# An encoder layer on one core: two blocks of the program made one, norm roots of eight token tiles taken ahead, and the last 32 tokens multiplied in four column tiles

## The chip, the cores and the metric

The kernel runs on one core of a Trainium2 chip. The metric is the device time of one execution in microseconds (us); lower is better. The hardware profiler recorded one execution, from which all rows below are taken.

## The reference, cut to what matters

Two sequences, a prompt of 256 tokens and a sample of 1024, each get 16 learned tokens in front and pass through one layer. All arithmetic is float32.

```
h = rmsnorm(x, norm1_g)
z = h @ w_in                      # u | q | k | v | o | gates
q, k = silu(centred_dwconv(q, k))
y_pool = pool_mixer(u)
h_f, h_b = mlstm_chunkwise forwards and backwards (q, k, v, gates)
h = (h_f + h_b) * rsqrt(mean((h_f + h_b)^2, per head) + EPS)
y_mlstm = h * mh_g * sigmoid(o)
x = x + [y_pool, y_mlstm] @ w_out
t = rmsnorm(x, norm2_g)
aff = softmax(t @ w_router); gate, idx = top_k(aff.T, cap)   # 16 experts
x = x + scatter_add(gate * ((silu(t[idx] @ w_gate) * (t[idx] @ w_up)) @ w_down))
return rmsnorm(x, final_g)
```

There are 4 heads of 192 columns, worked on in two passes of a pair (384 columns) each.

## The kernel before, in words

The two sequences lie one behind the other: 272 + 1040 = 1312 tokens (`LEN`), in `NT` = 11 tiles of 128 (`P`). Ten tiles are full; the last one, tile 10, has 32 tokens, and all products treat it as 128 wide. The order of the work is written out by hand, engine by engine; the engines meet at semaphores. The banks 0 to 2 of PSUM are handed out in turn by `bank_plan` (L75): whoever needs the next bank waits until the one that had it three places before is read out.

The program has three blocks, and at the end of a block every engine waits for all others.

**The first block** (L388 to L1169) has the input norm, the products with `w_in` and the two passes. On TensorE (PE):

- `output_gate` (L1007) multiplies each tile with the output-gate columns of the first pair and the 16 gate columns, 400 columns, 8 matmuls; `take_o` (L591) on ScalarE (ACT) copies the result, `gate_rows` (L1021) transposes the gates, and then come the products with the pool columns (L1053).
- `tokens_by_block` (L1079) gives v (and in the second pass first o) by token: for each of the 11 tiles 8 matmuls of 128 tokens by 384 columns. It stands in the program three times: v of pass 0, o of pass 1, v of pass 1. ACT copies each tile out of its bank (`evac`, L582). After v, PE waits until the last tile is read out, and starts the chain of chunk states (`transpose_keys`, `state_products`).
- Then the loop over the 11 chunks (L1136 to L1169). For each chunk VectorE (DVE) weighs the scores (L960), and PE multiplies them with v (L1167); DVE makes the hidden rows `hh` (L986, L989), ACT sums their squares (`square_hh`, L725), and GpSimd (POOL) multiplies them into `og` (L569).

After the last chunk of a pass the norm of the heads is taken for all tiles at once: ACT has summed the last squares, DVE makes the mean (L994), ACT the root (L794), DVE the reciprocal (L996):

```
square_hh(p, NT - 1)
act.wait_ge(ms_ready, p + 1)
act.activation(ss_h[:, :], ss_h[:, :], ACT.Sqrt).then_inc(rms_ready, 1)
```

**The second block** (L1172 to L1469) begins with the second pair's scaling by these reciprocals on POOL, a tile at a time in `ORDER_B` = 2, ..., 10, 0, 1 (L1207). Step n of its main loop on PE is: `project(n, 0)` (L1421, first 512 columns of the out projection, 8 matmuls of 128 by 512), the transposes of the normed tile n-1 (`transpose_t`) and of the mixer output of tile n+1 (`transpose_y`), the router logits of tile n-1 (L1418), and `project(n, 1)`. DVE adds the residual (`add`, L1281) and norms (`norm`, L1290), ACT moves transposes and squares. Between these, DVE does the rounds of the top-k search (`rank`, L1314), spread over the steps:

```
spread = {STEP_A + 1: (0, 0, 1, 5), STEP_A + 2: (0, 5, 6, 11), STEP_A + 3: (0, 11, 12, rounds),
          STEP_B + 1: (1, 0, 2, 7)}
```

with `STEP_A` = 5, `STEP_B` = 9 and `rounds` = 17. In step 8 of this table (tile 10, since `ORDER_B[8]` is 10) one round stands ahead of the add of the first half, and five ahead of the add of the second. After the loop DVE ends the search, and the rows of the first expert are gathered.

**The third block** (L1503 on) is the loop over the 16 experts. The change leaves it as it is.

Of the kernel before, what the change touches and what calls it, by code (L numbers as in the profile page):

```python
# [21 lines left out]
P = 128  # L22
D = 1024
# [10 lines left out]

GAP = 8
# [100 lines left out]
def encoder_program(nc, x_prompt, x_sample, meta, g1, w_in, conv_w, conv_b, gate_b, pool_w, pool_scale,  # L136
# [9 lines left out]
    with ctx:  # L146
# [160 lines left out]


# [79 lines left out]
        with nc.Block() as block:  # L388
# [103 lines left out]


            @block.gpsimd
            def _(pool):
# [48 lines left out]

                def mask_decay(p, i):
# [6 lines left out]
                for p in range(2):  # L552
# [17 lines left out]
                    pool.wait_ge(y_raw, (p + 1) * NT)  # L570
                    if p == 1:
                        break
                    pool.wait_ge(rs_ready, 1)
                    ogf = area("og", NT * PAIR).rearrange("p (n d) -> p n d", d=HD)
                    pool.tensor_tensor(ogf, ogf, ss_h[:, :].unsqueeze(2).to_broadcast([P, 2 * NT, HD]), ALU.mult).then_inc(y_scaled, 1)


            @block.scalar
            def _(act):
# [154 lines left out]

                gate_rows_first()
                for p in range(2):
                    for w in range(2):
# [14 lines left out]
                        if w == 0 and p:  # L752
                            act.wait_ge(y_out, 16)
                            for i in range(NT):
                                evac(("vo", p, i, 1), og[:, i, :, :], lambda b: b[:, 0:PAIR].rearrange("p (h d) -> p h d", h=2), ACT.Sigmoid)
                    if p == 0:
# [4 lines left out]
                    for i in range(NT):  # L761
                        b, k = plan[("vo", p, i, 0)]
                        if i == 0:
                            act.wait_ge(ones_set, 1)
                        evac(("vo", p, i, 0), v[:, i, :, 0:HD], lambda b: b[:, 0:PAIR].rearrange("p (h d) -> p h d", h=2))
# [5 lines left out]
                    for i in range(NT):  # L771
# [20 lines left out]
                    square_hh(p, NT - 1)  # L792
                    act.wait_ge(ms_ready, p + 1)
                    act.activation(ss_h[:, :], ss_h[:, :], ACT.Sqrt).then_inc(rms_ready, 1)  # L794


            @block.vector
            def _(dve):
                st = Steps(dve, dve_step)
                dve.memset(xin[NT - 1], 0.0).then_inc(x_clear, 1)  # L800
                dve.memset(small[:, 94:95], EPS).then_inc(eps_set, 1)
                dve.memset(gtok, 0.0).then_inc(zeroed, 1)
# [113 lines left out]

                def update_state(new, old, k0, k1, p, d, i):
# [14 lines left out]
                for p in range(2):  # L932
# [6 lines left out]
                    if p == 0:  # L939

                        b, k = plan[("rc", NT - 1)]
                        dve.wait_ge(full[b], k)
                        dve.memset(v[:, :, :, HD:VW], 1.0).then_inc(ones_set, 1)
# [6 lines left out]
                    for i in range(NT):  # L950
                        m = p * NT + i

# [870 lines left out]
```

## Time and profile before

| | |
|---|---|
| median of 3 runs | 1875.99 us (1874.95 to 1876.86) |
| the profiled execution | 1875.08 us, its span in the trace 1873.1 us |
| PE | busy 1795.1 us, 96% of the span |
| PE, weight loads | 1451.7 us, 77% |
| DVE | 472.4 us, 25% |
| ACT | 385.6 us, 21% |
| POOL | 210.5 us, 11% |
| mean granted TensorE clock | 0.981 |
| stages | first block to about 698 us, second to about 934 us, experts to the end |

How to read it: the kernel is float32, and each matmul of the program shows as two pairs of a weight load (PEld) and a matmul (PE) in the trace. A matmul's duration contains the way through the array, which the next one overlaps, so the pace of a row of matmuls is its whole time by their number. The granted clock is 1.00 at 2.4 GHz and 0.50 at 1.2 GHz. "<-" in brackets names who ended an engine's idle time, "issue" that nobody did in the records.

### The profile page before, as it was taken

Reading aid. Unit: us, or ns where it says so; the run is one execution under the profiler, and the core shown is the slowest. Engines: PE = TensorE matmul, PEld = TensorE weight load, DVE = VectorE, ACT = ScalarE, POOL = GpSimd, SP = SyncE. Lnnn points to the kernel's source line nnn. Section 1 sums busy time; section 2 is a strip of 40 time slices with the busy share of each in tenths; the row PEclk is TensorE's granted clock in tenths of the full one; section 3 lists DMA queues with packets and bytes.
Section 4 is the critical chain, followed back from the end, with each engine's and each line's share of the span. In section 5 each row is a group of like instructions: output and inputs, shape, how many; then the busy total and the mean of one; then the engine's idle time right before and its main releaser. Section 6 shows DMA issues by size and latency. Waiting matters only on the chain. (4 is left out here: it accounts for less than half of the span.)

```text
span 1873.1 us, 24252 instructions
## 1 busy us (share of the span) xinstructions
PE 1795.1 (96%) x10062; PEld 1451.7 (77%) x10062; DVE 472.4 (25%) x987; ACT 385.6 (21%) x868; POOL 210.5 (11%) x235
## 2 busy tenths in 40 slices
PE   7999999999999989999499999999999999999996
PEld 4555556955555774554299999999999999999995
DVE  3462103731020671156801101101111111111114
ACT  3335223633030551232100000000000000000005
POOL 0070010320100121000000111001110101110010
PEclk9999999999999999999689999999999999999998
DMA  6111111021100314433337686677776676876685
GB/s 193 49 48 28 40 34 40 24 85 34 34 29 1 130 44 136 170 113 131 123 123 270 218 292 223 222 245 256 249 266 218 229 269 223 283 240 214 231 283 204
DMA packets 149468, 292.28 MB, mean 156 GB/s; under 512 B 9193, under 2 KB 34457, under 8 KB 149413
## 3 DMA queue, kind: packets, MB, share of 16 engines
q1 hardware_dynamic: 142548, 269.35, 41.3%
q0 software_dynamic: 6864, 22.17, 4.7%
q8 instruction: 37, 0.61, 0.1%
q14 instruction: 19, 0.15, 0.0%
HBM read 260.20 MB, written 31.31 MB: 156 GB/s over the span
## 5 line engine op out<-in xcount | busy, mean ns | idle before, releaser
L1731 PE MATMUL bank<-arena 128*128 128x164 f32 x4096 | 581.1, 303 | 0.0
L1731 PEld LDWEIGHTS bank<-arena 128*128 128x128 f32 x4096 | 572.7, 190 | 0.3
L1750 PE MATMUL bank<-arena 128*128 128x164 f32 x2048 | 295.3, 303 | 0.0
L1750 PEld LDWEIGHTS bank<-arena 128*128 128x128 f32 x2048 | 286.5, 190 | 0.0
L1107 PE MATMUL bank<-arena 128*128 128x512 f32 (+1 forms) x576 | 215.2, 536 | 0.0
L1107 PEld LDWEIGHTS bank<-arena 128*128 128x128 f32 x576 | 110.3, 192 | 103.6 <-issue 93.6
L1640 DVE TENSOR_TENSOR arena<-bank,arena 128x328 f32<-128x328 f32 x64 | 32.0, 499 | 584.3 <-ACT arena L1580 584.3
L1085 PE MATMUL bank<-arena 128*128 128x384 f32 x528 | 171.2, 485 | 0.0
L1424 PE MATMUL bank<-arena 128*128 128x512 f32 x352 | 159.4, 611 | 1.1 <-issue 0.7
L1085 PEld LDWEIGHTS bank<-arena 128*128 128x128 f32 x528 | 99.8, 189 | 70.4
L1580 ACT ACTIVATE arena<-bank 128x328 f32<-128x328 f32 x64 | 28.4, 443 | 558.8 <-PE bank L1731 558.8
L1424 PEld LDWEIGHTS bank<-arena 128*128 128x128 f32 x352 | 67.6, 195 | 82.6 <-issue 82.4
L1546 POOL DMA_INDIRECT residual<-arena,cur_scatter x30 | 46.0, 1535 | 582.1 <-DVE arena L1648 577.5
L910 DVE SCALAR_TENSOR_TENSOR arena<-arena,par 128x272 f32<-128x272 f32 (+1 forms) x48 | 42.7, 931 | 234.9 <-ACT arena L687 234.5
L1588 ACT ACTIVATE arena<-bank 128x328 f32<-128x328 f32 x64 | 28.3, 443 | 280.1 <-PE bank L1750 280.0
L1636 DVE COPY arena<-bank 128x328 f32<-128x328 f32 x64 | 31.7, 495 | 196.5 <-PE bank L1714 196.5
L925 DVE SCALAR_TENSOR_TENSOR arena<-arena,spc,bank 128x193 f32<-128x193 f32 x120 | 42.7, 412 | 142.6 <-PE bank L1064 142.6
L1018 PE MATMUL bank<-arena 128*128 128x400 f32 x176 | 63.2, 512 | 0.7 <-DMA arena<-in_w_in 0.7
L1155 PE MATMUL bank<-arena 128*128 128x193 f32 x320 | 56.0, 326 | 0.0
L1018 PEld LDWEIGHTS bank<-arena 128*128 128x128 f32 x176 | 33.4, 195 | 24.8 <-issue 3.0
L585 ACT ACTIVATE arena<-bank 128x384 f32<-128x384 f32 (+1 forms) x50 | 25.5, 517 | 128.0 <-PE bank L1085 127.2
L1155 PEld LDWEIGHTS bank<-arena 128*128 128x128 f32 x320 | 51.8, 190 | 0.0
(210 smaller groups left out, 1427.0 us busy)
## 6 DMA issues: line engine op xcount, KB each, us to landing
arena<-in_w_up SPq DMA_DIRECT2D x32, 2048.0 KB, 12.7
arena<-in_w_down SPq DMA_DIRECT2D x32, 2048.0 KB, 10.4
arena<-in_w_gate SPq DMA_DIRECT2D x32, 2048.0 KB, 8.1
arena<-in_w_in SPq DMA_DIRECT2D x8, 1536.0 KB, 6.9
arena<-in_x_sample SPq DMA_DIRECT2D x14, 512.0 KB, 6.9
arena<-decay_rows SPq DMA_DIRECT2D x22, 256.0 KB, 3.7
residual<-arena SPq DMA_DIRECT2D x11, 512.0 KB, 5.3
ffn_in<-arena SPq DMA_DIRECT2D x11, 512.0 KB, 3.8
```

Of the source, the lines that this page charges most:

```text
L910: st.do(dve.scalar_tensor_tensor(o, Z[:, lo + n_seq + n_tap:hi + n_seq + n_tap], par[:, c0:c0 + 1], o, ALU.mult, ALU.add))
L925: last = dve.scalar_tensor_tensor(new[:, j, :], old[:, j, :], spc[:, a, i:i + 1], ps[b][:, c:c + VW], ALU.mult, ALU.add)
L1018: last = pe.matmul(ps[6 + i % 2][:, 0:OGW], hT[:, k, src], Wo[:, k, :], start=k == 0, stop=k == KT - 1)
L1085: last = pe.matmul(ps[b][:, 0:PAIR], hT[:, k, tile_cols(i)], Wb[nb % 2][:, k, :], start=k == 0, stop=k == KT - 1)
L1107: last = pe.matmul(ps[b][:, 0:hi - lo], Wb[nb % 2][:, k, j * P:(j + 1) * P], hT[:, k, lo:hi], start=k == 0, stop=k == KT - 1)
L1155: last = pe.matmul(ps[4 + half][:, h * VW:(h + 1) * VW], q, C, start=a == 0, stop=a == 1)
L1424: last = pe.matmul(ps[b][:, :], yT_t[n % 2][:, k * P:(k + 1) * P], wout[:, k, 512 * h:512 * h + 512], start=k == 0, stop=k == KT - 1)
L1546: pool.indirect_dma_start(out=acc_d[:, :], out_offset=bass.IndirectOffsetOnAxis(ap=cur_scatter[0:n, blk, :], axis=0), in_=yeS[0:n, blk, :] ...
L1636: dve.tensor_copy(xeT[:, 2 * m:2 * m + 2, :], gathered(None if first else e, m)[:, :, 0:SLOTS]).then_inc(t_done, 1)
L1640: dve.tensor_tensor(hidT[:, 2 * fp:2 * fp + 2, :], pair_of_tiles(2 + fp % 2), sil[:, fp % 2, :, :], ALU.mult).then_inc(hid_done, 1)
L1731: last = pe.matmul(ps[2 * w + fp % 2][:, a * SLOTS:(a + 1) * SLOTS], ring[2 * (fp // 2) + w][:, k, f * P:(f + 1) * P], xeT[:, k, :], start ...
L1750: last = pe.matmul(ps[4 + dp % 2][:, a * SLOTS:(a + 1) * SLOTS], ring[4 + dp // 2][:, k, dt * P:(dt + 1) * P], hidT[:, k, :], start=k == 0 ...
```

## The change

It does three things.

1. The first two blocks become one. Each engine goes on with its part of the out projection as soon as its own part of the passes is done, with the semaphores that stood there; three waits take the barrier's place (SP and ACT wait for `y_raw` to reach 22 before they use memory that the last chunk reads, POOL waits for `rs_ready`).
2. In pass 1 the norm roots of tiles 0 to 7 (`EARLY` = 8) are taken while the chunks 9 and 10 are still worked on: DVE makes their means ahead of chunk 9, ACT takes the root at the end of chunk 9, DVE the reciprocal ahead of chunk 10. POOL scales the first three tiles of the out projection (`HELD` = 3) ahead of the last chunk's product. The roots of tiles 8 to 10 follow as before, on ACT behind the copies of the first transposes (`last_norm(1)`).
3. The 32 tokens of tile 10 (`TAIL`) are multiplied in four column tiles of the array (`QUARTERS`). The stationary operand is the 32 tokens, and column tile g gives the g-th quarter of the columns, on partitions 32g to 32g+31. This is done in `output_gate` (100 columns a quarter), in the three `tokens_by_block` (96) and in both halves of `project` (128): 32 matmuls where there were 8. Whoever reads the bank does so in four pieces: ACT in `take_o` and `tail_out`, DVE in `add`. The unused 96 rows of `og` and `v` are set to zero once.

```diff
+TAIL = LEN - (NT - 1) * P
+QUARTERS = P // TAIL
...
+        EARLY = NT - 3
+        HELD = 3
...
+                def normed_gate(n):
+                    i = ORDER_B[n]
+                    pool.wait_ge(y_raw, NT + i + 1)
+                    pool.tensor_tensor(og[:, i, :, :], og[:, i, :, :], ss_h[:, 2 * i:2 * i + 2].unsqueeze(2).to_broadcast([P, 2, HD]),
+                                       ALU.mult).then_inc(y_scaled_b, 1)
...
+                        if p and i == NT - 1:
+                            pool.wait_ge(rs_ready, 2)
+                            for n in range(HELD):
+                                normed_gate(n)
...
+                for n in range(HELD, NT):
+                    if ORDER_B[n] == EARLY:
+                        pool.wait_ge(rs_ready, 3)
+                    normed_gate(n)
...
+                def tail_out(key, out, func):
+                    b, k = plan[key]
+                    act.wait_ge(full[b], k)
+                    w = PAIR // QUARTERS
+                    for g in range(QUARTERS):
+                        c = g * w % HD
+                        last = act.activation(out[0:TAIL, NT - 1, g * w // HD, c:c + w], ps[b][g * TAIL:(g + 1) * TAIL, 0:w], func)
+                    last.then_inc(free[b], 1)
...
+                    if ORDER_X[i] == NT - 1:
+                        w = OGW // QUARTERS
+                        for g in range(QUARTERS):
+                            hi = min(w, PAIR - g * w)
+                            act.activation(area("og", hi, TAIL, (NT - 1) * PAIR + g * w), src[g * TAIL:(g + 1) * TAIL, 0:hi], ACT.Copy)
+                        for r in range(2):
+                            last = act.activation(own_gates[0:TAIL, ORDER_X[i], r, :].rearrange("p (d n) -> p d n", n=4)[:, 0:NR // 4:BW // 4, :],
+                                                  src[P - TAIL:P, hi + 8 * r:hi + 8 * r + 8].rearrange("p (d n) -> p d n", d=2), ACT.Copy)
+                        last.then_inc(o0_free, 1)
+                        return
...
+                def last_norm(p):
+                    square_hh(p, NT - 1)
+                    act.wait_ge(ms_ready, 2 * p + 1)
+                    late = ss_h[:, 2 * EARLY * p:2 * NT]
+                    act.activation(late, late, ACT.Sqrt).then_inc(rms_ready, 1)
...
+                        if p and i == NT - 2:
+                            act.wait_ge(ms_ready, 2)
+                            act.activation(ss_h[:, 0:2 * EARLY], ss_h[:, 0:2 * EARLY], ACT.Sqrt).then_inc(rms_ready, 1)
...
+                halves("yT", 0, yT_t)
+                last_norm(1)
...
+                def mean_of(cols_):
+                    dve.tensor_scalar(ss_h[:, cols_], ss_h[:, cols_], 1.0 / HD, EPS, ALU.mult, ALU.add).then_inc(ms_ready, 1)
...
+                        if p and i == NT - 2:
+                            dve.wait_ge(hh_sq, 2 * (NT + EARLY))
+                            mean_of(slice(0, 2 * EARLY))
+                        if p and i == NT - 1:
+                            dve.wait_ge(rms_ready, 2)
+                            dve.reciprocal(ss_h[:, 0:2 * EARLY], ss_h[:, 0:2 * EARLY]).then_inc(rs_ready, 1)
...
+                    if ORDER_B[n] == NT - 1:
+                        w = 512 // QUARTERS
+                        for g in range(QUARTERS):
+                            c = slice(512 * h + g * w, 512 * h + (g + 1) * w)
+                            last = dve.tensor_tensor(x2[n % 2][0:TAIL, c], ps[b][g * TAIL:(g + 1) * TAIL, 0:w], x_t[n % 2][0:TAIL, c], ALU.add)
+                        last.then_inc(free[b], 1)
...
+                def tail_block(to, tokens, weights, w):
+                    for k in range(KT):
+                        for g in range(QUARTERS):
+                            last = pe.matmul(to[g * TAIL:(g + 1) * TAIL, 0:w], tokens(k), weights(k)[:, g * w:(g + 1) * w],
+                                             start=k == 0, stop=k == KT - 1)
+                    return last
...
-                    for k in range(KT):
-                        last = pe.matmul(ps[6 + i % 2][:, 0:OGW], hT[:, k, src], Wo[:, k, :], start=k == 0, stop=k == KT - 1)
+                    if ORDER_X[i] == NT - 1:
+                        last = tail_block(ps[6 + i % 2], lambda k: hT[:, k, LEN - TAIL:LEN], lambda k: Wo[:, k, :], OGW // QUARTERS)
+                    else:
+                        for k in range(KT):
+                            last = pe.matmul(ps[6 + i % 2][:, 0:OGW], hT[:, k, src], Wo[:, k, :], start=k == 0, stop=k == KT - 1)
...
+                        if i == NT - 1:
+                            tail_block(ps[b], lambda k: hT[:, k, LEN - TAIL:LEN], lambda k: Wb[nb % 2][:, k, :],
+                                       PAIR // QUARTERS).then_inc(full[b], 1)
+                            continue
...
-        with nc.Block() as block:
-            @block.sync
-            def _(sp):
...
+                    if ORDER_B[n] == NT - 1:
+                        w = 512 // QUARTERS
+                        for k in range(KT):
+                            for g in range(QUARTERS):
+                                last = pe.matmul(ps[b][g * TAIL:(g + 1) * TAIL, 0:w], yT_t[n % 2][:, k * P:k * P + TAIL],
+                                                 wout[:, k, 512 * h + g * w:512 * h + (g + 1) * w], start=k == 0, stop=k == KT - 1)
+                        last.then_inc(full[b], 1)
+                        return
```

The code of the old second block that is not shown moves into the first unchanged.

The order on PE at the end of pass 1, before (L1167 is the product with v, L1399 the transposes of the mixer output, L1424 the out projection):

```order
326 L1167 MATMUL bank<-arena 128x193 x4
327 L1140 MATMUL bank<-arena 128x128 x4
328 L1155 MATMUL bank<-arena 128x193 x4
329 L1167 MATMUL bank<-arena 128x193 x4
330 L388 UNCONDITIONAL_BRANCH
331 L1386 UNCONDITIONAL_BRANCH
332 L1399 MATMUL bank<-ident,arena 128x128 x8
333 L1424 MATMUL bank<-arena 128x512 x8
```

The same place of the change (L1461, L1434, L1449, L1476 and L1509 are these lines now):

```order
329 L1461 MATMUL bank<-arena 128x193 x4
330 L1434 MATMUL bank<-arena 128x128 x4
331 L1449 MATMUL bank<-arena 128x193 x4
332 L1461 MATMUL bank<-arena 128x193 x4
333 L1476 MATMUL bank<-ident,arena 128x128 x8
334 L1509 MATMUL bank<-arena 128x512 x8
```

PE issues the same, without the branches between the blocks.

ACT in chunks 9 and 10 of pass 1, as the change has it (L875 weighs the carried parts, L800 makes the decays, L812 the squares, L882 is the early root, L892 a copy of transposes, L819 the late root):

```order
276 L875 ACTIVATE arena<-bank,cols 128x193 x4
277 L800 ACTIVATE arena<-arena,cols 128x128 x4
278 L882 ACT_TABLE_LOAD
279 L882 ACTIVATE ss_h<-ss_h 128x16
280 L812 ACTIVATE arena,ss_h<-arena 128x192 x2
281 L875 ACTIVATE arena<-bank,cols 128x193 x2
282 L812 ACTIVATE arena,ss_h<-arena 128x192 x2
283 L892 ACTIVATE arena<-bank 128x512 x2
284 L812 ACTIVATE arena,ss_h<-arena 128x192 x2
285 L819 ACTIVATE ss_h<-ss_h 128x6
```

The table load for the root has moved ahead of the last two chunks' squares, and the copies of the first transposes ahead of the last chunk's squares.

POOL at the same place, as the change has it (L591 masks decays, L615 is the product into `og`, L584 the scaling; before, all 11 scalings stood behind the barrier):

```order
65 L615 TENSOR_TENSOR arena<-arena 128x384
66 L591 TENSOR_TENSOR arena<-arena,masks 128x512
67 L615 TENSOR_TENSOR arena<-arena 128x384 x2
68 L584 TENSOR_TENSOR arena<-arena,ss_h 128x384 x3
69 L615 TENSOR_TENSOR arena<-arena 128x384
70 L584 TENSOR_TENSOR arena<-arena,ss_h 128x384 x8
```

Three scalings now stand ahead of the last chunk's product.

## Rows read from the trace of the kernel before

**Rows 1.** The page: busy time of an engine, and the granted clock in 40 slices.
```profile
PE 1795.1 (96%) x10062; PEld 1451.7 (77%) x10062; DVE 472.4 (25%) x987; ACT 385.6 (21%) x868; POOL 210.5 (11%) x235
...
PEclk9999999999999999999689999999999999999998
```

**Rows 2.** Windows by stage: start:end, length, busy us and instructions of engines, granted clock, DMA.
```profile
698.00:707.00 9.00, 1.94 (x8) 1.57 (x8) 3.12 (x12) 3.46 (x8) 4.22 (x6) 0.63 0.00 0
707.00:934.00 227.00, 200.64 (x710) 108.62 (x710) 107.46 (x238) 49.77 (x100) 5.31 (x7) 0.93 0.40 139
```

**Rows 3.** Timeline, v of pass 0: start us, length us, engine, line, operation, shapes, count.
```profile
240.95 57.07 PE L1085 MATMUL bank<-arena 128*128 128x384 f32 x176
298.65 0.85 PE L1076 MATMUL bank<-ident,arena 128*128 128x128 f32 x6 [0.63 <-issue]
```

**Rows 4.** Timeline, the output gate of tile 10 and what follows it.
```profile
79.36 5.56 PE L1018 MATMUL bank<-arena 128*128 128x400 f32 x16
...
85.34 0.24 ACT L599 ACTIVATE arena<-bank 128x8 f32<-128x8 f32 x2
...
85.64 0.40 PE L1026 MATMUL bank<-ident,arena 128*36 128x128 f32 x2 [0.50 <-ACT arena L599]
```

**Rows 5.** Timeline, PE in one step of the state chain of pass 1.
```profile
619.86 0.56 PE L1062 MATMUL bank<-arena 128*128 128x193 f32 x2 [0.15 <-DVE arena L925]
620.35 0.38 PE L1063 MATMUL bank<-arena 128*64 128x193 f32 x1
620.36 0.38 PE L1064 MATMUL bank<-arena 128*64 128x193 f32 x1
...
620.83 0.59 PE L1066 MATMUL bank<-arena 128*128 128x193 f32 x2
```

**Rows 6.** Timeline, ACT in chunk 9 of pass 1: the decays.
```profile
690.39 1.27 ACT L721 ACTIVATE arena<-arena,cols 128x128 f32<-128x128 f32 x4
```

**Rows 7.** Timeline, from the last chunk of pass 1 to the out projection.
```profile
695.36 0.69 DVE L960 TENSOR_TENSOR arena<-bank,arena 128x512 f32<-128x512 f32 x1 [0.24 <-DVE arena L989]
...
696.11 1.58 PE L1167 MATMUL bank<-arena 128*128 128x193 f32 x8 [1.54 <-DVE arena L960]
...
701.49 1.28 ACT L794 ACT_TABLE_LOAD   x1
...
703.04 0.29 DVE L996 RECIPROCAL ss_h<-ss_h 128x22 f32<-128x22 f32 x1 [1.35 <-ACT ss_h L794]
...
704.57 1.94 PE L1399 MATMUL bank<-ident,arena 128*128 128x128 f32 x8 [6.88 <-POOL arena L1207]
707.25 8.72 PE L1424 MATMUL bank<-arena 128*128 128x512 f32 x16 [0.73 <-issue]
```

**Rows 8.** Timeline, PE in steps 7 to 9 of the out projection.
```profile
840.85 13.98 PE L1424 MATMUL bank<-arena 128*128 128x512 f32 x32
...
857.78 1.06 PE L1399 MATMUL bank<-ident,arena 128*128 128x128 f32 x8 [2.08 <-DVE arena L1286]
...
860.38 15.68 PE L1424 MATMUL bank<-arena 128*128 128x512 f32 x32
875.90 1.04 PE L1399 MATMUL bank<-ident,arena 128*128 128x128 f32 x8
```

**Rows 9.** Timeline, DVE: norm of step 7, first add and norm of step 8.
```profile
853.24 1.28 DVE L1296 SCALAR_TENSOR_TENSOR arena<-arena,small 128x1024 f32<-128x1024 f32 x1
...
856.94 0.69 DVE L1286 TENSOR_TENSOR arena<-bank,arena 128x512 f32<-128x512 f32 x1
...
872.78 1.28 DVE L1296 SCALAR_TENSOR_TENSOR arena<-arena,small 128x1024 f32<-128x1024 f32 x1
```

**Rows 10.** Windows around thin places on PE, columns as in rows 2.
```profile
385.00:388.50 3.50, 1.97 (x10) 1.73 (x11) 2.15 (x5) 1.53 (x6) 0.86 (x1) 1.00 1.00 363
...
860.00:864.00 4.00, 4.00 (x10) 1.99 (x10) 3.86 (x9) 0.18 (x1) 0.00 (x0) 0.59 0.00 0
```

**Rows 11.** Timeline, PE: the transposes of the gate rows of pass 0.
```profile
156.81 0.68 PE L1094 MATMUL bank<-ident,arena 36*128 36x36 f32 x8
```

More of the change, by code:

```diff
@@ L753, in _ @@
                             act.wait_ge(y_out, 16)
-                            for i in range(NT):
+                            for i in range(NT - 1):
                                 evac(("vo", p, i, 1), og[:, i, :, :], lambda b: b[:, 0:PAIR].rearrange("p (h d) -> p h d", h=2), ACT.Sigmoid)
+                            tail_out(("vo", p, NT - 1, 1), og, ACT.Sigmoid)
                     if p == 0:
@@ new lines, in _, with move, halves, exponentials @@
+                st = Steps(act, sem("act_step_b"))
+                def move(key, out, parts=P, w=512):
+                    multiplied(act, key)
+                    act.activation(out, ps[plan[key][0]][0:parts, 0:w], ACT.Copy).then_inc(free[plan[key][0]], 1)
+                def halves(name, n, slots):
+                    for h in range(2):
+                        move((name, n, h), slots[n % 2][:, 512 * h:512 * h + 512])
+                def exponentials(part):
+                    lo, hi = PARTS[part]
+                    act.wait_ge(soft_dve, part + 1)
+                    act.activation(L[:, lo:hi, :], L[:, lo:hi, :], ACT.Exp).then_inc(soft_act, 1)
@@ L797, in _ @@
+                exponentials(2)
+                affinities(3)
             @block.vector
@@ L1279, in _ @@
+                    late = slice(2 * EARLY * p, 2 * NT)
+                    mean_of(late)
+                    dve.wait_ge(rms_ready, 2 * p + 1)
+                    dve.reciprocal(ss_h[:, late], ss_h[:, late]).then_inc(rs_ready, 1)
                 st = Steps(dve, topk_step)
@@ new lines, in gate_rows @@
+                def gate_rows(i):
+                    pe.wait_ge(o0_free, i + 1)
+                    b = bank(("gt", i))
+                    for r in range(2):
+                        last = pe.transpose(ps[b][0:NR, r * P:(r + 1) * P], gtok[:, ORDER_X[i], r * NR:(r + 1) * NR], ident[:, :])
+                    last.then_inc(full[b], 1)
+                pe.wait_ge(ident_done, 1)
+                for i in range(NT):
+                    pe.wait_ge(xn_done, i + 1)
+                    for h in range(2):
+                        b = bank(("x", i, h))
+                        for k in range(4):
+                            c = (4 * h + k) * P
+                            last = pe.transpose(ps[b][:, k * P:(k + 1) * P], xn[i % 2][:, c:c + P], ident[:, :])
+                        last.then_inc(full[b], 1)
+                    if i:
+                        output_gate(i - 1)
+                    if i > 1:
+                        gate_rows(i - 2)
@@ new lines, in _ @@
+                output_gate(NT - 1)
+                gate_rows(NT - 2)
+                gate_rows(NT - 1)
+                pe.wait_ge(prow_in, 32)
+                b = bank(("par",))
+                pe.transpose(ps[b][:, 0:48], prow[0:48, :], ident[0:48, 0:48]).then_inc(full[b], 1)
+                pe.wait_ge(w_slot_in[1], 16)
+                for j in range(2):
+                    for c, (lo, hi) in enumerate(CHUNKS):
+                        b = bank(("u", j, c))
+                        for k in range(KT):
+                            last = pe.matmul(ps[b][:, 0:hi - lo], Wu[:, k, j * P:(j + 1) * P], hT[:, k, lo:hi], start=k == 0, stop=k == KT - 1)
+                        last.then_inc(full[b], 1)
```

455 lines of the change are left out of this document (204 added, 251 removed).

## The prediction

> **What bounds the kernel now.** I read the page first: PE is busy for 96% of the span, DVE for 25% [rows 1]. So whatever shortens PE's own work, or lets it begin earlier, counts one for one, unless another engine is late at that place. The windows by stage say where PE is not full: 1.94 us of the 9 between the first two blocks, and 200.6 of 227 in the second block, at a mean clock of 0.93 [rows 2]. In the first block the token products run without a gap, 176 passes (two for each matmul of the program) in 57.07 us [rows 3]. There the time is PE's. In the second block it is partly DVE's, which the timeline of step 8 must show.
>
> The sum is made against the profiled execution, 1875.08 us (span 1873.1 and 2.0 around it). It lies 0.9 us below the median of the runs, so I take what is saved from the median. A measurement of this kernel can tell about 0.2% (3.7 us) from no change.
>
> **The last tile's products.** A pass of 384 columns takes 57.07/176 = 0.324 us [rows 3], so a token tile of 16 passes takes 5.2 us. The output gate takes 5.56/16 = 0.347 us a pass, about 5.5 us [rows 4], half an out projection 13.98/2 = 7.0 us [rows 8]. With a quarter of the columns a pass is 0.081, 0.087 or 0.109 us long. The question is whether the four column tiles run beside each other. The state chain already has two: L1063 and L1064 use 64 of the array's columns each. They start 0.01 us apart, and both with their two passes are over when L1066 starts 0.48 us after them [rows 5]. Two passes of 193 columns alone need 2 x 0.324 x 193/384 = 0.33 us. So the two tiles do overlap, and going into the divided array and out of it costs 0.49 - 0.33 = 0.16 us (L1062 to L1063) and 0.48 - 0.33 = 0.15 us, 0.3 us in all.
>
> For four tiles I carry that over: 16 x 0.081 + 0.3 = 1.6 us for a token tile, 16 x 0.087 + 0.3 = 1.7 us for the gate, 16 x 0.109 + 0.3 = 2.05 us for half an out projection. The ends: 0.3 us less if four pieces hide the changes of shape; 64 passes one behind the other at the other end, 5.2 us, which is no gain, with a price on each change of tile as the loss (below). I take the near end, since rows 5 show the very form with two tiles. By the Trainium skill, TensorE: Matmul & The Clock Gate, Part 3, three column tiles measured 2.38 times the speed of one, four row tiles 3.07 times. By an estimate from that page, 5.2/3.07 = 1.7 us. The Trainium skill, TensorEngine Tiling (Array Packing), Key Properties, says that changing the tiling mode drains TensorE; the 0.3 us of rows 5 agree.
>
> What follows a tail on the path:
> - Output gate: the transposes of its gates wait for ACT's copies (0.50 us of waiting now [rows 4]). ACT now copies four quarters and two gate pieces. Copies follow each other at (1.27 - 0.40)/3 = 0.29 us for 128 columns [rows 6] and 0.12 us for 8 [rows 4], so 0.25 us for 96. Four end about 1.1 us after the product where one ended 0.5 us after it: 0.6 us more. Saved 5.5 - 1.7 - 0.6 = 3.2 us.
> - v of pass 0 and of pass 1: PE waits until the last tile is copied (0.63 us now [rows 3]), so 5.2 - 1.6 - 0.6 = 3.0 us each, 6.0 us.
> - o of pass 1: the next product needs another bank, the copies lie beside it. 5.2 - 1.6 = 3.6 us.
>
> Together 12.8 us. The zeroing of the unused rows lies on DVE beside PE's work and costs nothing; the cover is the wait for the first tile of x, and it would be 1 us if that cover went.
>
> **Blocks joined, roots early.** After the last product with v (L1167 at 696.11) PE waits 6.88 us before the first transposes at 704.57, and the out projection starts at 707.25 [rows 7]. In between lies the last chunk's chain: hidden rows, squares, mean, the table load of 1.28 us, root, reciprocal, the barrier, and the first scaling. Tile 2, the first of the out projection, needs none of the last chunk. After the change its root is ready two chunks ahead, and POOL's three scalings fit between its products for chunks 9 and 10. PE then goes on at 696.11 + 0.3 (the reciprocal that now stands ahead of L960 on DVE, 0.29 us as L996 [rows 7]) + 8 x 0.163 = 697.7. Transposes and copies took 2.68 us at half clock; at full clock the 8 transposes take 1.06 instead of 1.94 us [rows 7, 8], so 1.8 us. The out projection starts at 699.5, 7.7 us earlier. The table load moves to the end of chunk 9 on ACT. Behind it wait the squares of chunk 8 and the weighing of chunk 10, whose result DVE needs only after L1167; 1.5 us fit. Next late is the norm of step 0, which has two halves of a projection of time.
>
> The first projection took 8.72 us, where 7.0 us is its pace at full clock [rows 7, 8]: the granted clock of the stretch around the gap was 0.63 [rows 2]. If the clock holds after the change, 1.7 us more are saved. The last chunk of pass 0, with PE half idle but no transposes behind it, kept 1.00; the transposes and logits of step 8 were followed by 0.59 over 4 us [rows 10]. The new place has a part of each. I take the fall, so 7.7 us, with 9.4 as the upper end.
>
> **The out projection of tile 10.** PE's two halves shrink by 2 x (7.0 - 2.05) = 9.9 us, and I count none of it. The norm of step 7 ends on DVE at 853.24 + 1.28 = 854.5, after five rounds of the search; PE's first half now would end at 849.9 and wait for it. The second group of transposes already waits 2.08 us for DVE's first add of step 8 [rows 8, 9]. The norm of step 8 ends at 874.06 [rows 9], and PE starts on its transposes at 875.90 [rows 8]. The eight small adds in place of two cost DVE about 0.8 us (four at 0.29 us against 0.69 [rows 6, 9]), so these transposes come at 874.9 at best: 1.0 us gained. Against it, PE has waits of about 5 us in steps 8 and 9, and a fall of the clock costs 4 x (1 - 0.59) = 1.6 us each [rows 10]. Bounds +1.0 and -3.4 us; I take 0.
>
> **Sum:** 12.8 + 7.7 + 0 = 20.5 us. 1875.99 - 20.5 = 1855.5 us. Its own range is 1849.5 to 1860: upwards if two falls more come, downwards if the clock holds (1.7), the copies hide (1.8), the changes of shape too (1.2), and 1.0 comes from step 8.
>
> **Rivals.**
> 1. *PE cannot feed the small passes.* 64 passes with 64 weight loads must be issued where there were 16. The fastest pace the trace shows over several passes is (0.68 - 0.23)/7 = 0.064 us [rows 11]. At that pace a tail takes 64 x 0.064 + 0.3 = 4.4 us: 0.8 us are left at o, 0.2 at each v, 0.5 at the gate, in all 1.7 + 7.7 = 9.4 us, 1866.6 us. For it: nothing faster lasts anywhere. Against it: the two tiles of rows 5 start within 0.01 us. The Trainium skill, TensorE: Matmul & The Clock Gate, Part 1, gives 62 ns a matmul spent in PE's sequencer in one of its decode settings; by that rule the tails would come out as in this rival, and the pace of rows 11 agrees, though its loads of 128 columns can explain it too. Chance 0.20.
> 2. *The clock falls behind the tails.* Each tail leaves a thin stretch (waits for copies, small transposes). A fall after the gate, both v and in step 8 costs 4 x 1.7 = 6.8 us: 1862.3 us. For it: rows 10. Against it: the state chain follows v at once, and it kept full clock. Chance 0.15.
> 3. *Slower than before: each change of column tile drains the array.* Then 64 passes follow each other (5.2 us) and 32 changes cost 0.15 us each, 10 us for a tail of 5.2. Three token tiles lose 16 us with their copies, the gate 6, the two halves in step 8 about 7 beyond DVE's lag, and the joined blocks give back 7.7: +21 us, 1897 us. It decides from about 0.035 us a change with no overlap. Rows 5 speak against it, since one change from L1063 to L1064 cost 0.01 us. Chance 0.03.
> 4. *The gain of tile 10's projection comes through,* because DVE's rounds are late only by waiting on PE: 9.9 us more, 1845.6 us. The rounds follow each other without a gap, so 0.03.
>
> The forecast has 0.55; 0.04 is left for no change or something unseen.
>
> **Range and chances.** 1849 to 1867 us holds the forecast and rivals 1 and 2 with their centres; what is outside (rivals 3 and 4, the far tails) is under 0.2. Faster by over 0.2%: 0.95. Within: 0.02. Slower: 0.03.
>
> **What would show it.** Tails of 1.6 to 2 us with four matmuls started within 0.03 us; 4.4 us means rival 1, 10 us rival 3. The first out projection about 1.8 us behind the last product with v, its 16 passes in 8.7 or 7.0 us. In steps 8 and 9 idle PE ended by DVE's norm or add, and the transposes of tile 10 no more than about 1 us earlier against the start of the out projection. The experts' stage unchanged at 929 us. I am wrong in kind if the gap between the old blocks is still over 3 us, or if the step of tile 10 is shorter by more than 3 us.

## The result, and the profile after

| | before | the change |
|---|---|---|
| median | 1875.47 us (4 runs, 1874.51 to 1876.86) | 1851.24 us (4 runs, 1849.99 to 1852.36) |
| ratio, 95% interval | | 0.9872 (0.9860 to 0.9884) |
| span of the profiled execution | 1873.1 us | 1849.8 us |

The change is 24.2 us faster. The forecast was 20.5 us faster, with 1855.5 us and a range of 1849 to 1867; the measured time lies inside. The page of after answers to rows 1:

```profile
PE 1772.4 (96%) x10350; PEld 1446.4 (78%) x10350; DVE 476.2 (26%) x999; ACT 388.1 (21%) x881; POOL 210.0 (11%) x235
...
PEclk9999999999999999998599999999999999999998
```

PE has 288 passes more (six tails with 48 each) and is busy for 22.7 us less. Each digit of the clock row is a slice of about 46 us. The lowest one (6 before, 5 now) is the end of the second block in both, 890 to 937 us before and 879 to 925 now. The 8 in front of it, 832 to 879 us, is new: it holds step 8 of the out projection. The gap at the joint was too short to show in such a slice.

**The tails.** The timeline of after, PE, at the output gate of tile 10 (rows 4), v of pass 0 (rows 3), o, and v of pass 1:

```profile
78.02 1.58 PE L1290 MATMUL bank<-arena 128*32 128x100 f32 x64
79.54 0.40 PE L1316 MATMUL bank<-ident,arena 128*36 128x128 f32 x2
80.86 0.40 PE L1316 MATMUL bank<-ident,arena 128*36 128x128 f32 x2 [0.92 <-ACT arena L672]
...
287.70 1.53 PE L1290 MATMUL bank<-arena 128*32 128x96 f32 x64
290.40 0.85 PE L1366 MATMUL bank<-ident,arena 128*128 128x128 f32 x6 [1.17 <-issue]
...
484.36 1.53 PE L1290 MATMUL bank<-arena 128*32 128x96 f32 x64
485.82 1.55 PE L1401 MATMUL bank<-arena 128*128 128x512 f32 x3
...
590.59 1.53 PE L1290 MATMUL bank<-arena 128*32 128x96 f32 x64
593.29 0.85 PE L1366 MATMUL bank<-ident,arena 128*128 128x128 f32 x6 [1.17 <-issue]
```

All 64 passes of a token tail end within 1.53 us. The next product behind o starts 1.46 us after the tail did, where a full tile takes 5.2 us. The last piece of waiting, 1.17 us (0.63 in rows 3), is ACT's four copies, which the timeline gives as 1.00 us together:

```profile
289.30 1.00 ACT L654 ACTIVATE arena<-bank 32x96 f32<-32x96 f32 x4 [0.99 <-PE bank L1290]
```

**The joint of the blocks.** The same timeline, PE, where rows 7 stood before:

```profile
682.32 1.58 PE L1461 MATMUL bank<-arena 128*128 128x193 f32 x8 [1.56 <-DVE arena L1125]
683.74 1.03 PE L1476 MATMUL bank<-ident,arena 128*128 128x128 f32 x8
685.56 7.10 PE L1509 MATMUL bank<-arena 128*128 128x512 f32 x16 [0.79 <-issue]
```

The 6.88 us of waiting before the transposes are gone, the projection starts 3.24 us behind the last product with v (11.14 before), and runs at full clock: 7.10 us where rows 7 have 8.72.

**Step 8 of the out projection.** The timeline, PE, where rows 8 stood:

```profile
824.57 1.95 PE L1504 MATMUL bank<-arena 128*32 128x128 f32 x64
831.27 1.97 PE L1476 MATMUL bank<-ident,arena 128*128 128x128 f32 x8 [4.74 <-DVE arena L1188]
834.95 1.94 PE L1476 MATMUL bank<-ident,arena 128*128 128x128 f32 x8 [1.72 <-DVE arena L1175]
836.68 3.43 PE L1495 MATMUL bank<-arena 128*128 128x16 f32 x16
840.05 3.64 PE L1504 MATMUL bank<-arena 128*32 128x128 f32 x64
843.62 7.41 PE L1509 MATMUL bank<-arena 128*128 128x512 f32 x16
851.79 0.44 PE L1476 MATMUL bank<-ident,arena 128*128 128x128 f32 x2 [0.75 <-DVE arena L1188]
```

PE waits three times for DVE (4.74, 1.72, 0.75 us). In the windows of after (start:end, length, busy us and instructions, granted clock, DMA) the clock is at 1.2 GHz from the end of the first wait, about 830.5 us, to about 844.5:

```profile
595.00:598.50 3.50, 3.50 (x15) 2.22 (x15) 1.16 (x3) 0.94 (x3) 0.00 (x0) 0.51 1.01 411
830.50:844.50 14.00, 11.51 (x98) 10.20 (x99) 13.50 (x30) 2.57 (x5) 0.00 (x0) 0.51 0.33 121
```

The first of these two rows is a new, short fall behind v of pass 1, which the profile of before doesn't have.

The experts' stage is unchanged: 932.2 us before (from 940.96 us on) and 932.4 us now (from 917.39 us on).

### The profile page after: what moved, and what is told of

Read it like the earlier page. It is cut to its first block and busy times, and to the rows that moved or that the text cites. A ratio compares the mean times of both kernels' runs of the same rounds, so it can differ in the third digit from the quotient of the medians.

```text
span 1849.8 us, 24844 instructions
## 1 busy us (share of the span) xinstructions
PE 1772.4 (96%) x10350; PEld 1446.4 (78%) x10350; DVE 476.2 (26%) x999; ACT 388.1 (21%) x881; POOL 210.0 (11%) x235
## 5 line engine op out<-in xcount | busy, mean ns | idle before, releaser
L1816 PEld LDWEIGHTS bank<-arena 128*128 128x128 f32 x4096 | 572.8, 190 | 0.3
L1835 PEld LDWEIGHTS bank<-arena 128*128 128x128 f32 x2048 | 286.5, 190 | 0.0
L1401 PEld LDWEIGHTS bank<-arena 128*128 128x128 f32 x576 | 109.8, 191 | 102.8 <-issue 92.9
L1379 PE MATMUL bank<-arena 128*128 128x384 f32 x480 | 155.7, 485 | 0.0
L1509 PE MATMUL bank<-arena 128*128 128x512 f32 x320 | 142.7, 602 | 1.1 <-issue 0.8
L1379 PEld LDWEIGHTS bank<-arena 128*128 128x128 f32 x480 | 90.8, 189 | 63.9
L1509 PEld LDWEIGHTS bank<-arena 128*128 128x128 f32 x320 | 60.5, 193 | 73.2 <-issue 73.0
L1308 PE MATMUL bank<-arena 128*128 128x400 f32 x160 | 56.3, 504 | 0.5 <-DMA arena<-in_w_in 0.5
L1449 PE MATMUL bank<-arena 128*128 128x193 f32 x320 | 56.0, 326 | 0.0
L1449 PEld LDWEIGHTS bank<-arena 128*128 128x128 f32 x320 | 51.8, 190 | 0.0
L1733 DVE TENSOR_SCALAR arena<-bank,gatec 128x512 f32<-128x512 f32 (+1 forms) x60 | 44.3, 738 | 12.4 <-PE bank L1847 12.4
```

The source lines that it names most:

```text
L1308: last = pe.matmul(ps[6 + i % 2][:, 0:OGW], hT[:, k, src], Wo[:, k, :], start=k == 0, stop=k == KT - 1)
L1379: last = pe.matmul(ps[b][:, 0:PAIR], hT[:, k, tile_cols(i)], Wb[nb % 2][:, k, :], start=k == 0, stop=k == KT - 1)
L1401: last = pe.matmul(ps[b][:, 0:hi - lo], Wb[nb % 2][:, k, j * P:(j + 1) * P], hT[:, k, lo:hi], start=k == 0, stop=k == KT - 1)
L1449: last = pe.matmul(ps[4 + half][:, h * VW:(h + 1) * VW], q, C, start=a == 0, stop=a == 1)
L1509: last = pe.matmul(ps[b][:, :], yT_t[n % 2][:, k * P:(k + 1) * P], wout[:, k, 512 * h:512 * h + 512], start=k == 0, stop=k == KT - 1)
L1733: dve.tensor_scalar(yeS[0:n, blk, 512 * h:512 * h + 512], ps[7][0:n, :], gatec[0:n, blk, bass.ds(e, 1)], None, ALU.mult).then_inc(o_done, 1)
```

## Experiments

Each gain is given against the median of the kernel before, timed in the same rounds on the same chip.

### The two halves of the change: e2, e3

```diff
 # e2: all products and readers of tile 10 in their 128-wide form; joint and early roots stay
-                    if ORDER_X[i] == NT - 1:
+                    if False:
                         last = tail_block(...)
... (the same at the other products and readers)
```

> Only the joined blocks and the early roots; all products of tile 10 are 128 wide as before. My theory (the terms are separate and add up; the joint is worth 8 to 9.4 us, the tails the rest): 8.5 us under the kernel before, about 1867 us, out projection starting 7 to 8 us nearer to the last chunk of pass 0 than before, and its first 16 passes at full clock in 7.0 us. Rival (the clock holds at the joint only because the tails changed the load ahead of it): the first 16 passes take 8.7 us again and the gain is 7 us or less.

e3 is the kernel before with `tail_block`, `tail_out`, the tail forms of `take_o`, `add` and `project`, and the zeroing; blocks and roots as before.

> Only the tails; the two blocks stay apart and all roots are taken after the last chunk, as before. My theory: 13.3 us from gate, o and twice v, 0 to 1 from step 8, so 13.5 us under the kernel before, about 1862 us, with the wait of 6.9 us before the first transposes still there and the first out projection at half clock for a part (8.7 us). Rival (the projection of tile 10 is worth a part of its 9.9 us, and the joint less than its 8): 16 us or more under the kernel before.

| | median | before | gain | ratio (95%) |
|---|---|---|---|---|
| e2, joint and roots only | 1867.55 | 1876.83 | 9.3 us | 0.9952 (0.9939 to 0.9965) |
| e3, tails only | 1860.29 | 1876.83 | 16.5 us | 0.9914 (0.9902 to 0.9927) |

The gains add up to 25.8 us, the change has 24.2. In e2 the first 16 passes take 7.11 us, so the clock at the joint holds without any tail: its rival falls.

```profile
697.90 7.11 PE L1505 MATMUL bank<-arena 128*128 128x512 f32 x16 [0.79 <-issue]
```

In e3 the wait and the slower first projection are both back:

```profile
684.94 1.58 PE L1212 MATMUL bank<-arena 128*128 128x193 f32 x8 [1.53 <-DVE arena L990]
693.40 1.94 PE L1451 MATMUL bank<-ident,arena 128*128 128x128 f32 x8 [6.88 <-POOL arena L1252]
696.07 8.98 PE L1484 MATMUL bank<-arena 128*128 128x512 f32 x16 [0.73 <-issue]
```

The median of e3 lies 3 us beyond what I expected (the interval is 13.7 to 18.4 us), at its rival's figure; the profiled spans differ by 13.3 us (1873.1 against 1859.8), as expected. That agreement is partly luck: e3's profile has a fall of the clock behind both v (about 1.1 us each), and lacks one at the end of the out projection (its last half takes 7.11 us, where before has 8.81). The medians alone don't exclude a few us from tile 10's projection; e1 below looks at that.

### Barrier or roots: e4, e5

```diff
 # e4: blocks joined, all roots of pass 1 late, nothing scaled ahead of the last chunk
-        EARLY = NT - 3
-        HELD = 3
+        EARLY = 0
+        HELD = 0
...
-                halves("yT", 0, yT_t)
                 last_norm(1)
+                halves("yT", 0, yT_t)
```

> The change with its blocks joined, but the roots of pass 1 all taken after the last chunk, and no scaling ahead of it. My theory (the chain squares, mean, table load, root, reciprocal, scaling is what PE waited for, the barrier adds only 0.3 to 1 us to it): PE waits 5.9 to 6.6 us before the first transposes, the clock falls there again, and the run is 6 to 8 us slower than the change, about 1858 us. Rival (the barrier was the cost): within 2 us of the change, at 1853 us or less.

e5 is e3 with the early mean, root, reciprocal and the three early scalings of the change put in.

> Tails and early roots with three tiles scaled ahead of the last chunk, but the two blocks apart. My theory: the barrier now waits for the last chunk's squares, mean, root and reciprocal, so PE still waits about 4.7 us (6.9 less the table load of 1.3 and the first scaling of 0.9), 5 to 7 us slower than the change, about 1857 us; neither part alone gives much, both together give 8. Rival (early roots carry it, the barrier costs little): PE waits under 2 us, within 2 us of the change.

| gain, us | all roots late | early roots |
|---|---|---|
| blocks apart | 16.5 (e3) | 16.1 (e5) |
| blocks joined | 14.9 (e4) | 24.2 (the change) |

e4's ratio is 0.9917 (0.9904 to 0.9930), e5's 0.9922 (0.9909 to 0.9935). Neither part alone gives anything that can be measured; both together give some 8 us. The timelines show what each leaves. e4, then e5:

```profile
681.74 1.58 PE L1447 MATMUL bank<-arena 128*128 128x193 f32 x8 [1.54 <-DVE arena L1111]
689.97 1.94 PE L1462 MATMUL bank<-ident,arena 128*128 128x128 f32 x8 [6.65 <-issue]
692.64 10.07 PE L1495 MATMUL bank<-arena 128*128 128x512 f32 x16 [0.73 <-issue]
```

```profile
683.47 1.58 PE L1240 MATMUL bank<-arena 128*128 128x193 f32 x8 [1.57 <-DVE arena L1017]
689.98 1.94 PE L1479 MATMUL bank<-ident,arena 128*128 128x128 f32 x8 [4.93 <-PEq L392]
692.65 8.73 PE L1512 MATMUL bank<-arena 128*128 128x512 f32 x16 [0.73 <-issue]
```

Without the barrier the wait is 6.65 in place of 6.88 us, since the chain to the root is what takes the time: in e4 DVE starts the reciprocal at 688.67 us, POOL the first scaling at 689.04, PE its transposes at 689.97. With early roots and the barrier it is 4.93 us (PEq L392 is PE's sequencer at the barrier), since the barrier waits for the last chunk's squares and root, which the first transposes don't need: in e5 the reciprocal of the late tiles starts at 689.31 us, and PE goes on at 689.98. Either wait lets the clock fall, 1.6 to 3.0 us more on the first projection; that makes e4 9.3 us slower than the change, more than the 6 to 8 expected.

### Do the column tiles overlap: e6, e10

```diff
 # e6, in tail_block and project
-                    for k in range(KT):
-                        for g in range(QUARTERS):
+                    for g in range(QUARTERS):
+                        for k in range(KT):
```

> The change with the loops of the tail exchanged: all 8 matmuls of one column tile, then those of the next, so that neighbours in the order share a column tile. My theory (column tiles overlap because neighbours in the order go to different ones): each tail takes 64 passes of 0.081 us, about 5.3 us where 1.6 were, 3.6 us more at each of gate, v, o, v, in all 12 to 15 us slower than the change, about 1865 us. Rival (passes on one column tile alone are just as quick, since the columns and not the overlap set the pace): the same as the change within 1 us.

```diff
 # e10
-QUARTERS = P // TAIL
+QUARTERS = 2
...
-to[g * TAIL:(g + 1) * TAIL, 0:w]
+to[2 * g * TAIL:(2 * g + 1) * TAIL, 0:w]
```

> The change with the last tile in two column tiles (0 and 2, half of the columns each) in place of four. My theory (the overlapped tiles share the pace of one wide product, so the pass is as long as the columns of one tile need): 16 pairs of 0.16 us, a token tail of 2.6 us against 1.53, with two copies fewer, 3 to 4 us slower than the change. Rival (passes are set by how fast they are issued, or each column tile has a speed of its own of 0.07 us per 96 columns): token tail of 2.3 us or less, within 2 us of the change.

The v tail of pass 0 in e6, then the gate's tail of e10, from their timelines:

```profile
290.62 4.57 PE L1290 MATMUL bank<-arena 128*32 128x96 f32 x64
296.33 0.85 PE L1366 MATMUL bank<-ident,arena 128*128 128x128 f32 x6 [1.15 <-issue]
```

```profile
79.70 2.91 PE L1290 MATMUL bank<-arena 128*32 128x200 f32 x32
```

e6 is at 1864.84 us, before at 1875.76: 10.9 us of gain, 13.3 less than the change (ratio 0.9942, 0.9928 to 0.9956), within the 12 to 15 expected. The same 64 passes take 4.57 us when neighbours share a column tile and 1.53 us when they alternate, a factor of 3.0. Against the full tile's 5.2 us it is 3.4. By the Trainium skill, TensorE: Matmul & The Clock Gate, Part 3, three column tiles and four row tiles measured 2.38 and 3.07 times the speed of one. It has no figure for four column tiles; the trace's 3.0 and 3.4 are of the same size.

With two tiles (e10: 1856.84, before 1876.75, ratio 0.9897, 0.9882 to 0.9912) a pair of 200-column passes takes 2.91/16 = 0.18 us, against 1.58/16 = 0.10 us for four of 100 columns in the change, the last one's way through the array in both. A v tail takes 2.79 us (2.6 expected), and the kernel is 4.9 us slower than the change on the same chip (e11), where I had 3 to 4. So the time goes with the columns of one tile's pass, and more tiles in flight cut it.

### Tile 10's projection: e1, e7, e8, e9, e11

e1 makes `project` and `add` of tile 10 128 wide again. e7 takes the change and places the search anew; e8 is e7 with the wide projection; e9 goes further.

```diff
 # e7
-STEP_A + 3: (0, 11, 12, rounds),
+STEP_A + 3: (0, 11, 11, 12), STEP_B: (0, 12, 13, 15),
...
                         softmax(1, n - 1)
+                        rank(0, 15, rounds)
 # e9: a fifth number, rounds between the second add and the norm
+spread = {STEP_A + 1: (0, 0, 1, 5, 6), STEP_A + 2: (0, 6, 6, 10, 10), STEP_A + 3: (0, 10, 10, 11, 12),
+          STEP_B: (0, 12, 13, 14, rounds), STEP_B + 1: (1, 0, 1, 5, 6)}
...
                     add(n, 1)
+                    if n in spread:
+                        rank(part, r2, r3)
                     norm(n)
```

> The change with the out projection of tile 10 (product and add) 128 wide again; everything else as in the change. My theory (DVE's rounds of the search hide it): 0 to 1 us slower than the change, 1851 to 1852 us, although PE works 9.9 us more at full clock; the half clock of step 8 goes with it. Rival (the gain comes through): 5 to 10 us slower than the change, 1856 to 1861 us.

> The change with the rounds of the search of part 0 placed anew: step 8 has one (behind its first add) where it had six, step 9 has five more (one ahead of its first add, two behind it, two behind the softmax). Nothing is left out. My theory (step 8 is set by DVE, and its PE time is free): PE idles 3 to 4 us less, the clock stays up for another 3 to 5, in all 5 to 9 us faster than the change, about 1844 us. Rival (the norm's own chain behind the add sets step 8, not the rounds): under 2 us.

> As the one before, with the out projection of tile 10 128 wide again. My theory: with the rounds out of the way PE sets step 8, and the wide projection costs 6 to 10 us more than the narrow one, where it cost 0 to 1 with the rounds in place. Rival (projection hidden in either case): within 2 us of the one before.

> The change with the rounds of the search placed so that none stands ahead of a norm that PE waits for: step 7 has four where it had six, step 8 two where it had six (one of them in DVE's wait for the squares), step 9 five; steps 6, 9 and 10 have one each in that wait of 1.6 to 2.9 us. Nothing is left out. My theory (DVE's backlog ahead of the transposes of steps 7 and 10 is the rest of the wait): PE's wait behind the first half of tile 10 falls from 4.75 to about 2.5 us, the one behind add 10 from 3.0 to under 1, 4 to 7 us faster than the change, about 1846 us. Rival (the rest of the wait is the chain add, square, root, norm itself, and the end of the search is set by DVE's sum of work): 3 us faster than the change or less, as with the rounds moved before.

> The change itself once more, with its profile, beside the two others on the same chip. It shows how far the profiled execution moves by falls of the clock alone: I expect 1851 us within 2 us, the tails at 1.5 us again, and one fall more or less behind v (1.1 us) or in the out projection (1.7 us).

| | median | before | gain | ratio (95%) |
|---|---|---|---|---|
| e1, wide projection | 1854.25 | 1875.76 | 21.5 us | 0.9885 (0.9870 to 0.9900) |
| e7, rounds moved | 1848.82 | 1875.76 | 26.9 us | 0.9852 (0.9838 to 0.9865) |
| e8, rounds moved, wide | 1854.13 | 1875.76 | 21.6 us | 0.9883 (0.9868 to 0.9898) |
| e9, rounds in the norms too | 1844.69 | 1876.75 | 32.1 us | 0.9826 (0.9813 to 0.9840) |
| e11, the change again | 1851.95 | 1876.75 | 24.8 us | 0.9866 (0.9851 to 0.9881) |

With the rounds in place the narrow projection is worth 24.2 - 21.5 = 2.7 us by the medians, whose intervals overlap, where I had 0 to 1. The timelines say less: from the start of the out projection to the transposes of tile 10 e1 takes 167.0 us (688.14 to 855.17) and the change 166.2 (685.56 to 851.79). So 0.8 us, out of 9.9 of PE's own time. The transposes of tile 10 in e1:

```profile
855.17 2.20 PE L1476 MATMUL bank<-ident,arena 128*128 128x128 f32 x16
```

With the rounds moved it is worth 5.3 us (e7 against e8), still less than the 6 to 10 expected. e7 itself gains 2.7 us on the change (the intervals touch), where I had 5 to 9; its timeline shows why:

```profile
825.04 1.95 PE L1505 MATMUL bank<-arena 128*32 128x128 f32 x64
831.75 3.55 PE L1477 MATMUL bank<-ident,arena 128*128 128x128 f32 x16 [4.75 <-DVE arena L1188]
835.13 1.86 PE L1496 MATMUL bank<-arena 128*128 128x16 f32 x16
836.92 1.95 PE L1505 MATMUL bank<-arena 128*32 128x128 f32 x64
```

I had moved the rounds of step 8, but the first wait is for the norm of step 7, which stands behind step 7's rounds. e9 takes two rounds out of step 7:

```profile
827.57 1.96 PE L1508 MATMUL bank<-arena 128*32 128x128 f32 x64
831.76 2.25 PE L1480 MATMUL bank<-ident,arena 128*128 128x128 f32 x16 [2.23 <-DVE arena L1188]
833.84 1.86 PE L1499 MATMUL bank<-arena 128*128 128x16 f32 x16
835.62 1.95 PE L1508 MATMUL bank<-arena 128*32 128x128 f32 x64
```

The wait is 2.23 us (2.5 expected). A later one, behind the add of step 10, is 0.74 us, where e7 has 3.02 and the change 1.36 (under 1 expected). e9 is 7.3 us faster than the change on the same chip (e11), with intervals apart; I had 4 to 7. The windows over the stage, the change and then e9, show PE's busy time falling with the half clock, 0.89 to 0.92, at equal numbers of passes:

```profile
685.50:917.40 231.90, 194.24 (x808) 110.15 (x808) 111.30 (x255) 50.97 (x104) 9.23 (x11) 0.89 0.40 139
```

```profile
688.50:910.90 222.40, 188.82 (x808) 105.61 (x808) 111.17 (x255) 50.87 (x104) 9.25 (x11) 0.92 0.42 145
```

### The fall of the clock behind v: e12

The windows of 8 us from the first key transpose on, behind v of pass 0 and of pass 1, in the change:

```profile
290.40:298.40 8.00, 7.03 (x41) 4.39 (x41) 3.20 (x9) 3.40 (x10) 3.22 (x3) 1.00 0.58 163
593.30:601.30 8.00, 7.34 (x36) 4.72 (x37) 2.46 (x7) 2.82 (x8) 0.00 (x0) 0.79 0.97 380
```

The row with 0.79 belongs to a pass in which the time from there to the last product with v is 1.1 us longer (89.03 us, 87.88 before). In the nine profiles with four alternating column tiles at the end of v (the change, e1, e3, e4, e5, e7, e8, e9, e11), 13 of 18 such places show 0.79; e4 shows it in neither. In the four that don't have them there (before, e2 wide, e6 one tile after the other, e10 two tiles) it is 1.00 in all 8. The wait before the transposes doesn't do it alone. e6 has the same one (1.15 us, where the change has 1.17), behind a tail that doesn't overlap, and its clock holds behind both v:

```profile
296.30:304.30 8.00, 6.99 (x41) 4.41 (x41) 3.20 (x9) 3.37 (x10) 3.23 (x3) 1.00 0.59 163
605.30:613.30 8.00, 7.03 (x42) 4.35 (x42) 3.20 (x9) 3.44 (x10) 0.00 (x0) 1.00 0.97 373
```

Nor does the tail: behind the one of o, which full products follow, the clock is 1.00 over the next 8 us in all nine profiles. e12 takes e9 and puts tile 10 first in v:

```diff
+V_ORDER = (NT - 1,) + tuple(range(NT - 1))
...
-                    for i in range(NT):
+                    for i in range(NT) if w else V_ORDER:
                         b = bank(("vo", p, i, w))
... (the plan of banks, ACT's copies and the waits for the last tile of v follow the new order)
```

> The kernel with the rounds in the norms, and in both v products tile 10 comes first in place of last, so that its small passes stand between full work and a full tile is the last that PE waits for. Nothing is left out. My theory (the falls of the clock behind v come from the thin stretch tail, wait, transposes, and the wait of 1.17 us is four copies in a row): granted clock 1.00 in the 8 us behind both v, the wait back at 0.6 us, so 0.5 us twice and up to 1.1 us twice, 1 to 3.5 us faster than with the rounds in the norms alone, ratio about 0.981. Rival (the falls have nothing to do with where the tail stands): 0.79 there in one or both again, within 1.2 us.

```profile
293.40:301.40 8.00, 7.00 (x41) 4.41 (x41) 3.20 (x9) 3.38 (x10) 3.23 (x3) 1.00 0.59 164
596.00:604.00 8.00, 7.03 (x43) 4.35 (x43) 3.20 (x9) 3.45 (x10) 0.00 (x0) 1.00 0.93 346
```

The clock holds in both, and where the tails now stand (1.00 from 238 to 246 us, and from 541 to 549), and the wait is back at 0.63 us. The median is 1840.16, before 1874.71, a gain of 34.6 us against e9's 32.1; the intervals (0.9799 to 0.9826, and 0.9813 to 0.9840) overlap, so the 2.5 us are not shown by time. e12 is the fastest kernel of the study. In pass 0 it gives part back, since the fourth product wants tile 10's bank before ACT has copied it out (ACT had the sigmoid of the output gate to do first, 246.47 to 250.19 us):

```profile
251.15 41.33 PE L1386 MATMUL bank<-arena 128*128 128x384 f32 x127 [1.11 <-ACT arena L657]
```

## Why the prediction was right

The mechanism was right in its main parts: what the tails save, what the joint saves, and why tile 10's projection gives next to nothing. Two judgements on the clock were wrong, and by luck they work against each other: it held at the joint (1.6 us gained) and fell behind v (1.1 us lost). The terms, measured in the profiled executions from a landmark ahead of each place to one behind it:

| term | forecast | measured | from |
|---|---|---|---|
| gate | 3.2 | 3.4 | 79.36 to 85.64 before, 78.02 to 80.86 after |
| v of pass 0 | 3.0 | 3.2 | 240.95 to 298.65, 235.88 to 290.40 |
| v of pass 1 | 3.0 | 3.2 | 550.54 to 608.23, 538.76 to 593.29 |
| o | 3.6 | 3.6 | 440.79 to 497.70, 432.54 to 485.82 |
| joint | 7.7 | 7.9 | 696.11 to 707.25, 682.32 to 685.56 |
| clock at the joint | 0 (up to 1.7) | 1.6 | 8.72 and 7.10 |
| rest of the out projection | 0 (+1.0 to -3.4) | 0.3 | 233.7 and 231.8 from its start to the experts, less the row above |
| clock behind v | 0 (rival 2: -1.7 each) | -1.1 | one fall, pass 1 |

That is 22.1 us. The change's execution also reached its first tail 1.3 us earlier than before reached the product there (78.02 against 79.36); with it the sum is 23.4, the spans' 23.3. These 1.3 us are scatter and no part of the change: in e11, the same kernel, the tail starts at 79.32. The interval of the median's gain goes from 21.8 to 26.3 us. The 22.1 lies inside it, the forecast's 20.5 does not; the difference is the 1.6 us of the joint's clock, and the rest of the deviations cancel.

- **The tails.** The two tiles of rows 5 were the right base for four: 1.53 and 1.58 us where I had 1.6 and 1.7, and 1.95 where I had 2.05 (the first half; the second ran at half clock, 3.64). At o 1.46 - 16 x 0.081 = 0.16 us is left for the changes of shape, where I had 0.3. The copies cost what I took for them, 0.25 us each. Four passes start within 0.02 us, 7 ns apart.
- **The joint.** The transposes came 1.42 us behind the last product's start, where I had 1.3. The 0.3 us that I had added for the reciprocal ahead of L1125 don't show: e2 takes 87.9 us from the first key transposes to this product, as before. Where I chose, between a clock that falls and one that holds, I took the fall, and it holds in every kernel of the study without the wait (the change, e1, e2 and e6 to e12), and falls in all with it (e3, e4, e5). That was the mis-sized term: 0 in the sum, 1.6 measured.
- **Tile 10's projection.** 0 to 1 us by the timelines, and DVE's norm and adds end the waits, as forecast. I had priced a fall there at 1.6 us; it lasts some 14 us, but DVE is busy for 13.50 of the 14.00 us of that window, and even at half clock PE waits for it at the end of them (0.75 us). So it is DVE and not PE's pace that sets the time. The eight small adds cost DVE 0.98 us more than the two they replace (1.18 a half against 0.69); by my own price of 0.29 they would have been 0.94, where I wrote 0.8.
- **Rival 1** (PE cannot feed the passes) is excluded: 64 passes in 1.53 us are 0.024 us each, under the 0.064 it took. By the Trainium skill, TensorE: Matmul & The Clock Gate, Part 1, a matmul costs 62 ns of sequencer with hardware decode off; by an estimate from that figure a tail would take 64 x 0.062 = 4.0 us. The trace's 1.53 us show that this rule did not bind here.
- **Rival 2** (the clock falls behind the tails) is partly true, and my argument against it, that the state chain kept full clock before, was wrong: it does not always keep it behind an alternating tail. But the price at v is 1.1 us and not 1.7, the gate showed no fall (1.00 from 80 to 88 us), and the one in step 8 lies beside DVE's work.
- **Rival 3** (changes of tile drain): e6, with few changes of tile, is slower and not faster.
- **Rival 4** (tile 10's projection comes through) needs DVE's rounds out of the way, and then gave 5.3 us.
- **The range.** By the terms I named, its own ends are 1849.8 and 1858.9, not 1849.5 and 1860.

## What to carry to other kernels

A ragged tile of 32 rows is worth splitting by columns over four column tiles, with the tiles alternating in the innermost loop; price it as the wide product's time by four, plus 0.2 to 0.3 us for the changes of shape and one short copy per tile for the reader (0.25 us each here). Where two things end at the same wait (a barrier and a chain of small operations), measure both removed before judging either: here each alone gave nothing and both gave 8 us. Time saved on an engine shows only as far as the other engine's work in that step, and the norm that it waits for, are moved too.

## What the runs showed that I had not expected

- On one 32-wide column tile a pass of 96 columns takes (4.57 - 0.245)/63 = 0.069 us (0.245 is a single one's length), 0.72 ns a column, where full-width passes take 0.324/384 = 0.84 ns a column.
- The clock fell behind v only where v ended in four alternating tiles, in 13 of 18 places, and not always in the same pass of the same kernel: the change had one fall in its first profile and two in e11's. The wait behind the tail is not enough by itself (e6, two places), nor is the alternating tail (the one of o, and e12's), so wherever it fell there were both. Two places of e6 are few, and why it falls in some executions and not in others stays open.
